# Sixteen weight tiles of the even input projection rounded by ScalarE instead of GpSimd

## The reference, cut to what matters

```
proj = (h @ w_in)                       # 1024 -> 2560: q, k, v, g, xr, xg
q, k = rope(q), rope(k)
ret_out = silu(g) * head_rms(retention_chunked(q, k, v))
lru_out = rg_lru(causal_conv(xr)) * gelu(xg)
x = x + concat(ret_out, lru_out) @ w_out
x = x + square(relu(rmsnorm(x) @ w_up)) @ w_down
```

## Time and profile before

| what | value |
|---|---|
| median of 3 runs | 2465.09 us (2463.67 to 2467.01) |
| profiled execution, its own time | 2467.69 us |
| its span, first to last instruction | 2465.9 us |
| TensorE matmul busy | 2430.1 us, 99% |
| VectorE busy | 1388.4 us, 56% |
| GpSimd busy | 1003.2 us, 41% |
| ScalarE busy | 792.5 us, 32% |
| mean granted TensorE clock | 0.995 |

### The profile page before, as it was taken

How to read it: one execution, slowest core, us unless ns; L and a number is a source line. 1 busy time by engine, 2 the same in 40 slices (tenths; PEclk the granted TensorE clock), 3 DMA queues, 4 the chain that set the end, 5 groups by cost and what they waited for, 6 DMA issues and landing times. The chain is left out here.

```text
span 2465.9 us, 40868 instructions
## 1 busy us (share of the span) xinstructions
PE 2430.1 (99%) x15934; PEld 2383.1 (97%) x15934; DVE 1388.4 (56%) x2082; ACT 792.5 (32%) x1244; POOL 1003.2 (41%) x751
## 2 busy tenths in 40 slices
PE   8999999999999999999999999999999999999997
PEld 8999999999999999999999999999999999999997
DVE  6974366345545545567666666556345545445576
ACT  4711442222223223223344454442222122122233
POOL 2343124364554555473101111134364564464571
PEclk9999999999999999999999999999999999999999
DMA  4123031111111111111311111131111111111112
GB/s 149 35 63 89 25 125 45 43 44 43 52 52 42 46 51 43 52 52 41 120 42 58 51 45 55 34 126 49 46 44 43 53 44 43 52 48 39 52 53 80
DMA packets 40010, 140.09 MB, mean 57 GB/s; under 512 B 6208, under 2 KB 9920, under 8 KB 38560
## 3 DMA queue, kind: packets, MB, share of 16 engines
q1 hardware_dynamic: 32192, 104.55, 13.0%
q10 hardware_dynamic: 7648, 33.04, 3.7%
HBM read 120.46 MB, written 14.88 MB: 55 GB/s over the span
## 5 line engine op out<-in xcount | busy, mean ns | idle before, releaser
L716 PE MATMUL PS<-RB,WH 128*128 128x384 f32 (+1 forms) x4368 | 1085.6, 330 | 6.8 <-issue 6.8
L716 PEld LDWEIGHTS PS<-RB,WH 128*128 128x128 f32 x4368 | 770.8, 189 | 15.6 <-issue 12.7
L716 PE MATMUL PS<-RA,WH 128*128 128x272 f32 (+2 forms) x3520 | 770.5, 309 | 11.7 <-DVE RA L1809 10.4
L716 PE MATMUL PS<-RB,WL 128*128 128x384 f32 (+1 forms) x2232 | 730.6, 327 | 0.0
L716 PEld LDWEIGHTS PS<-RA,WH 128*128 128x128 f32 x3520 | 588.1, 188 | 16.2 <-issue 11.8
L716 PE MATMUL PS<-RA,WL 128*128 128x272 f32 (+2 forms) x1760 | 541.1, 307 | 0.0
L622 POOL TENSOR_TENSOR WH<-WR,FEW 128x1024 fp32r<-128x1024 f32 x106 | 204.8, 1932 | 775.4 <-PE PS L716 750.6
L716 PEld LDWEIGHTS PS<-RB,WL 128*128 128x128 f32 x2232 | 420.3, 188 | 0.0
L716 PEld LDWEIGHTS PS<-RA,WL 128*128 128x128 f32 x1760 | 331.2, 188 | 0.0
L1908 DVE TENSOR_TENSOR X<-PS,X 128x544 f32<-128x544 f32 x280 | 202.5, 724 | 203.7 <-PE PS L716 203.7
L1849 DVE SCALAR_TENSOR_TENSOR RAW<-PS,RS 128x384 f32<-128x384 f32 (+1 forms) x192 | 97.2, 532 | 350.0 <-PE PS L716 321.4
(11 more groups left out here) (225 smaller groups left out, 2375.7 us busy)
## 6 DMA issues: line engine op xcount, KB each, us to landing
WR<-ws SPq DMA_DIRECT2D x189, 512.0 KB, 3.3
X<-xT ACTq DMA_DIRECT2D x8, 544.0 KB, 8.0
EB<-xT ACTq DMA_DIRECT2D x8, 544.0 KB, 5.6
x_spill<-X ACTq DMA_DIRECT2D x1, 4352.0 KB, 15.2
EB<-x_spill ACTq DMA_DIRECT2D x8, 544.0 KB, 7.0
GA<-st_gla ACTq DMA_DIRECT2D x4, 1024.0 KB, 5.1
glas_o<-GA ACTq DMA_DIRECT2D x4, 1024.0 KB, 3.9
yT<-X SPq DMA_DIRECT2D x16, 208.0 KB, 1.9
```

Of the source, the lines that this page charges most:

```text
L716: return nc.tensor.matmul(out, lhsT, rhs, start=start, stop=stop, skip_group_check=True)
```

## The change

Tiles 4 to 19 are rounded by ScalarE and only subtracted by GpSimd. GpSimd's loop over tiles 4 to 31 is cut in two: tiles 4 to 19 take `low_part`, which waits for `w_high` and subtracts, and tiles 20 to 31 take `parts` as before. Tiles 0, 2 and 3 stay with GpSimd, and tile 1 was ScalarE's already. ScalarE's walk through the even list gets a new step: at the first group (or its first half) of step u, ahead of whatever it does for that item and behind all it does for the items before, it waits for the load of tile u+1 and for the end of step u-1, and copies `WR` to `WH`. Ahead of tile 4 it also waits until tile 3 is split. `next_high` is moved up to serve both layers.

```
+HIGH_EVEN = range(B_EVEN_IN + 4, B_EVEN_IN + 20)
...
-            with pool.Fori(2, (B_MLP0 + 4) // 2) as i:
+            with pool.Fori(HIGH_EVEN[0] // 2, HIGH_EVEN[-1] // 2 + 1) as i:
+                for slot in range(2):
+                    low_part(2 * i + slot, slot)
+            with pool.Fori(HIGH_EVEN[-1] // 2 + 1, (B_MLP0 + 4) // 2) as i:
                 for slot in range(2):
                     parts(2 * i + slot, i, slot, False)
...
+            def next_high(n):
+
+                act.wait_ge(w_loaded[n % 2], 16 * (n // 2) + 16)
+                act.wait_ge(gemm_done, 6 * n - 6)
+                A(WH[:, n % 2, :], WR[:, n % 2, :], ACT.Copy).then_inc(w_high, 1)
+
             for item in even:
                 kind = item[0]
+                if kind == "S" and item[2] == 0 and item[3:] != (1,) and item[1] + 1 in HIGH_EVEN:
+                    if item[1] + 1 == HIGH_EVEN[0]:
+
+                        act.wait_ge(w_split, HIGH_EVEN[0])
+                    next_high(item[1] + 1)
```

More of the change, by code:

```diff
@@ L1636, in _ @@
             act.dma_start(x_spill, X[:, :, :]).then_inc(x_spilled, 16)
[L1638 to L1642, removed]
             for item in odd:
```

## The result

The changed kernel takes 2475.24 us (median of six runs, 2474.78 to 2479.75); the kernel before, run beside it, 2466.34 (six runs, 2463.67 to 2467.92). The ratio is 1.0042, 95% interval 1.0031 to 1.0052: slower by 8.9 us from median to median. The profiled execution of the changed kernel took 2474.80 us with a span of 2473.0.

The account below looks back on a forecast made before the run. TensorE, busy 2430.1 of 2465.9 us, was taken to bound the kernel. A stall of 6.3 us plus 1.6 of slow clock, 7.9, on a median of 2465.1 gave 2473.0 us; own range 2469.9 to 2477.3, widened to 2469.0 to 2477.5.

Parts of the forecast that it names:

- The place: Before step 15: tile 15's rounding stands behind DECAY in ScalarE's queue, so GpSimd and then TensorE wait; stall 6.3 us.
- Tile 10's copy: ScalarE, end of step 8: copy goes ahead of the last L2 item's Sqrt, which starts at 137.9, ahead of VectorE; cost 0.
- The size of the stall: TensorE before step 15: 8.8 us if DECAY ends where it did, 6.3 with gains of 1.7 and 0.85.
- VectorE's relief of 1.7 us: VectorE's small multiplication before the first `decay_done`: without GpSimd's rounding beside it, DECAY comes 1.7 us earlier, bounds 0 and 1.7.
- The gain of 0.85 us in the DMA issues: DECAY's first eight DMA issues: SP's tile load no longer beside them, so one slow issue shortens; bounds 0 and 0.85.
- The clock: TensorE behind the stall before step 15: half clock after idling adds 1.6 us, bounds 0 and 3.4.
- The sum: Whole kernel: 6.3 of stall plus 1.6 of clock, 7.9 us slower, 2473.0 us.
- At most 1.76 us could be won: Even mixer's window: TensorE busy 303.24 of 305 us, so its idle time limits any gain to 1.76 us.
- the one of no relief (stall 8.8): Rival at step 15: DECAY ends no earlier, 8.8 + 1.6 = 10.4 us, time 2475.5 us; chance 15%.
- More than one stall: Rival in the retention: copies of tiles 17 to 19 delay key and value copies, at most 3.2 us more, 2476.2; 7%.
- Not slower: Rival in step 14: ScalarE free of DECAY by 202.9, so tile 15 isn't held up; 2465.1 or 2463.3 us; 10%.

Follow-up runs that it names:

- experiment 1: Changed kernel with ScalarE's copy of tile 15 moved into DECAY, ahead of the sixteen moves; 2466.79 us, ratio 0.9999 to the kernel before.
- experiment 2: Changed kernel with tile 15 given back to GpSimd, the other fifteen staying with ScalarE; 2465.17 us, ratio 0.9994 to the kernel before.
- experiment 3: Changed kernel with only tile 15 rounded by ScalarE, behind DECAY, and GpSimd rounding the other fifteen; 2474.51 us, ratio 1.0035 to the kernel before.
- experiment 6: Changed kernel plus one GpSimd copy of tile 15 into the free WL slot at step 14's start; 2474.50 us, ratio 1.0036.
- second session: Changed kernel run again unaltered, giving its second profile; 2473.35 us against 2465.47 for the kernel before, ratio 1.0034.

## Why the prediction was right

*The place* was right, and experiments 1, 2 and 3 show it from both sides: with tile 15 moved or given back the loss is gone, with tile 15 alone it is there. So were the steps around it. Tile 10's copy held ScalarE until the end of step 8, and the Sqrt of the last L2 item came at 138.16 (forecast 137.9), still ahead of VectorE, which reached that item at 140.52 (forecast 139.8 or later; L1543 of the changed kernel is L1528 of before, and L2170 is L2161):

```profile
138.16 1.11 ACT L1543 ACTIVATE X<-X 128x1088 f32<-128x1088 f32 x1
...
140.52 0.06 DVE L2170 MEMSET X<- 128x1 f32 x1
```

*The size of the stall* was forecast as 6.3 and measured as 6.6 and 6.4, but by two terms of which one holds.
- VectorE's relief of 1.7 us holds, by experiment 6 (8.0 against 6.4). Before, the first `decay_done` memset stood at 197.06, now at 195.57, in a stage that stood 0.2 us later.
- The gain of 0.85 us in the DMA issues did not come, and its cause was wrong. SP's load is no longer beside the moves, and still one issue took 1.71 us (durations ns min/median/max of the eight):

```profile
L1558 ACTq DMA_DIRECT2D X<-EB x8: 601/612/1712, 195.8 to 201.3; - x8
```

  What does lie beside it is one packet on a queue that the profile calls the instruction queue, in the window 199 to 200:

```profile
q8 instruction: 1, 0.02, 8.1%
```

  All nine profiles have one such packet, between 199.1 and 200.8. In eight of them the issue during which it came, one of the first eight, took 1.32 to 2.02 us. In experiment 3 it came during the last of the first eight. None of those was long, the next issue took 0.90, and the stall was 0.8 us shorter, 5.8:

```profile
L1558 ACTq DMA_DIRECT2D X<-EB x8: 601/612/613, 196.0 to 200.5; - x8
L1562 ACTq DMA_DIRECT2D EB<-EB x8: 612/612/903, 201.1 to 205.9; - x8
```

  That ScalarE waited there for its instructions fits all nine, but no run separates it, and it stays open. The Trainium skill (DMA: Bandwidth & Descriptors, "Issuing engines are not separate DMA queues") says that DMAs of all issuing engines interleave on the same 16 DMA engines, and it names no cost to another engine's issue. By it alone the 0.85 was not to be had, and the measurement agrees.
- A little came from elsewhere. The sixteen issues took 11.35 us in place of 11.48 (to 207.11, before to 208.74), and the two loads went out 1.90 us behind the last of them in place of 2.14. With VectorE's 1.7 that is 2.1 us of relief where 2.55 were forecast: 8.8 - 2.1 = 6.7 is the stall that was measured, 6.6.

*The clock* was the other mis-sized term: 1.6 forecast, 1.7 to 2.9 measured. I had read one start, where the part of the half clock behind it was short; it gave about the least of what the five stalls show. The bounds, 0 and 3.4, held.

*The sum* of 7.9 us stands against 8.9 and, in the second session, 7.9 between medians. That the latter agrees to the tenth is in part luck, as the clock cost 2.9 us in one profile of this code and 1.7 in the other; the time of 2475.24 lies in the range, 2.2 above the forecast, of which 1.25 is the median of before, 2466.34 in place of 2465.09. One premise was too narrow. "At most 1.76 us could be won" counts TensorE's idle time alone; the same 305 us hold half clock too, here at 312:

```profile
312.00:314.00 2.00, 1.90 (x8) 1.21 (x7) 1.97 (x3) 2.00 (x4) 0.00 (x0) 0.50 0.80 256
```

It lasts 6.8 us in all nine profiles, so it bears on no difference here.

Of the rivals, the one of no relief (stall 8.8) was wrong for the reason that experiment 6 gives. "More than one stall" was right in kind and too large in size. A new wait on ScalarE's copy of a result late in the mixer appears:

```profile
PE PS L720 <- ACT X L1592: 1.1, 1, 1.1
```

A wait of 0.9 or 1.1 us on that copy is in five of the seven profiles in which ScalarE rounds tiles 17 to 19. It is not in the kernel before or in experiment 3, where GpSimd rounds them. It isn't in the second profile of the changed kernel, and the fast experiment 2 has it. From the end of the ruler's stage to an idle stretch that all nine share (it ends at 651.39 before and at 661.55 after), the profiles with it are 0.3 to 0.8 us longer, which lies within the spread of the times. The forecast had put this at 0. "Not slower" was wrong because ScalarE was not free of DECAY by 202.9, but at 209.84. With experiment 1's order it would have been right.

## What to carry to other kernels

Before an instruction with a deadline is put into an engine's queue, list what stands ahead of it there for every instance, DMA issues and waits for landings among them; the mean load of the engine (here 32%) says nothing of the one instance in sixteen that is late. In this kernel, whose matmul engine is busy 99% of the time, a single stall of 4 to 8 us cost its length and 1.7 to 2.9 us of slow clock on top. Here the copy could go ahead of the batch of DMA issues without a measurable cost (experiment 1).

## What I had not expected of the hardware

ScalarE issued DMAs while its own copy was running: the copy at 195.27 for 1.06 us and the first issue at 195.28 (experiment 1). And the cost of the slow clock did not follow the length of the stall: 2.5 us behind a stall of 4.2, 1.7 behind one of 6.4, with some 6.8 us at half clock in both. The longer stall had used up more of them while TensorE was idle.
